# Moving the MLP's first-product weight tiles 128 bytes down in SBUF, and one slot of the other operand 384 up

## The reference, cut to what matters

```python
x = x + rms_norm(y, post_mix_norm_w[layer])
h2 = rms_norm(x, pre_mlp_norm_w[layer])
a = jax.nn.relu(jnp.einsum("bsd,df->bsf", h2, w_ff1[layer]))
m_out = jnp.einsum("bsf,fd->bsd", a * a, w_ff2[layer])
x = x + rms_norm(m_out, post_mlp_norm_w[layer])
```

## Time and profile before

| what | us |
|---|---|
| median of the runs | 2107.64 |
| the two runs | 2107.47, 2107.82 |
| span of the profiled execution | 2109.4 |
| PE busy in it | 2065.3 |
| first product, from its first matmul to the second product's first | 628.4 |
| second product, to the end of its last matmuls | 613.4 |

### The profile page before, as it was taken

One profiled execution on the slowest core, in us unless ns is written; L12 is line 12 of the kernel. 1 busy time (PEld: TensorE's weight loads), 2 busy tenths in 40 slices (PEclk: granted clock), 3 DMA queues, 4 the chain that ended last, 5 costly groups with the idle time before them and its releaser, 6 DMA issues. The chain is left out here.

```text
span 2109.4 us, 26456 instructions
## 1 busy us (share of the span) xinstructions
PE 2065.3 (98%) x9843; PEld 1719.6 (82%) x9843; DVE 1441.5 (68%) x1979; ACT 913.2 (43%) x1545; POOL 414.6 (20%) x252
## 2 busy tenths in 40 slices
PE   7999999999999999899999999999999999999998
PEld 4897878878788888688888788888788888888887
DVE  5797999989567777876667866666663536534286
ACT  5633334343445444655445644554432313313163
POOL 0000000000001322333322322332262144400012
PEclk9999999999999999999999999999999999999999
DMA  5031212113656865854455655445766455443376
GB/s 201 11 101 51 70 40 77 54 30 107 195 165 205 264 225 167 269 175 136 153 164 179 235 165 157 138 145 172 254 227 249 163 206 187 167 167 137 140 250 219
DMA packets 253118, 338.53 MB, mean 160 GB/s; under 512 B 11584, under 2 KB 193600, under 8 KB 239168
## 3 DMA queue, kind: packets, MB, share of 16 engines
q1 hardware_dynamic: 220352, 315.80, 44.9%
q10 hardware_dynamic: 32384, 20.98, 3.1%
q0 software_dynamic: 256, 0.07, 0.0%
HBM read 225.58 MB, written 111.21 MB: 160 GB/s over the span
## 5 line engine op out<-in xcount | busy, mean ns | idle before, releaser
L1861 PE MATMUL psum<-x_hi,w_hi_P 128*128 128x512 f32 x896 | 350.5, 391 | 12.3 <-DVE x_lo L1805 6.2
L2079 PE MATMUL psum<-w_hi,hid_hi 128*128 128x512 f32 x896 | 349.3, 390 | 2.0 <-DVE hid_lo L1957 2.0
L1861 PE MATMUL psum<-x_lo,w_hi_P 128*128 128x512 f32 x896 | 349.6, 390 | 0.0
L1861 PE MATMUL psum<-x_hi,w_lo_P 128*128 128x512 f32 x896 | 349.5, 390 | 0.0
L2079 PE MATMUL psum<-w_lo,hid_hi 128*128 128x512 f32 x896 | 349.3, 390 | 0.0
L2079 PE MATMUL psum<-w_hi,hid_lo 128*128 128x512 f32 x896 | 349.1, 390 | 0.0
L1957 DVE TENSOR_TENSOR hid_lo<-hid_raw,hid_hi 128x1024 fp32r<-128x1024 f32 x112 | 176.7, 1615 | 207.4 <-ACT hid_hi L1952 207.3
L1774 POOL TENSOR_TENSOR w_raw<-w_raw 128x512 f32<-128x512 f32 x128 | 181.5, 1439 | 410.7 <-DVE w_lo_P L1787 388.5
L1952 ACT ACTIVATE hid_hi<-hid_raw 128x1024 fp32r<-128x1024 f32 x112 | 113.0, 1051 | 342.6 <-DMA hid_raw<-scratch_hid 342.6
L1787 DVE TENSOR_TENSOR w_lo_P<-w_raw,w_hi_P 128x512 fp32r<-128x512 f32 x224 | 184.6, 836 | 107.2 <-ACT w_hi_P L1783 104.2
L1783 ACT ACTIVATE w_hi_P<-w_raw 128x512 fp32r<-128x512 f32 x224 | 136.8, 627 | 255.7 <-PE psum L1861 249.3
(11 more groups left out here) (280 smaller groups left out, 3762.0 us busy)
## 6 DMA issues: line engine op xcount, KB each, us to landing
scratch_hid<-stage SPq DMA_DIRECT2D x224, 256.0 KB, 3.6
hid_raw<-scratch_hid SPq DMA_DIRECT2D x56, 1024.0 KB, 4.9
w_raw<-in_w SPq DMA_DIRECT2D x52, 1024.0 KB, 5.0
w_grain<-in_w SPq DMA_DIRECT2D x48, 512.0 KB, 5.0
x_raw<-scratch_h2s SPq DMA_DIRECT2D x14, 1024.0 KB, 8.5
w_raw<-in_w_in SPq DMA_DIRECT2D x22, 512.0 KB, 3.6
scratch_h2s<-h2s SPq DMA_DIRECT2D x8, 1280.0 KB, 9.2
scratch_qk<-qout ACTq DMA_DIRECT2D x16, 512.0 KB, 3.0
```

The lines of the kernel that those rows point to most:

```text
L1861: mm = nc.tensor.matmul(psum[:, bank_1(op, g), :], l, r, start=kt == 0 and i == 0, stop=kt == 3 and i == 2)
L2079: mm = nc.tensor.matmul(psum[:, bank, :], l, r, start=f == 0 and k == 0, stop=f == NFP - 1 and k == 2)
```

## The change

Two numbers of the placement change. The 14 weight tiles of the first product move down by 1/8 KB, to remainder 0 modulo 512. Slot 7 of the tokens moves up by 3/8 KB, to remainder 0 as well; its high, low and raw tiles move together. The other seven slots and everything else stay. The tiles' order, sizes and contents are the same, and so are all instructions, waits and transfers on every engine, in number and in order.

```diff
-    x_at = [203.5, 0, 32, 16, 48, 105, 121, 167]
+    x_at = [203.5, 0, 32, 16, 48, 105, 121, 167 + 3 / 8]
     x_hi = [at(f"x_hi{i}", kb, (4, TB), F32R) for i, kb in enumerate(x_at)]
     x_lo = [at(f"x_lo{i}", kb + 8, (4, TB), F32R) for i, kb in enumerate(x_at)]
     x_raw = [at(f"x_raw{i}", kb + 8, (4, TB)) for i, kb in enumerate(x_at)]
-    w1_hi = {op: at(f"w1_hi_{op}", 69 + 2 * i, (4, P), F32R) for i, op in enumerate(OPS)}
-    w1_lo = {op: at(f"w1_lo_{op}", 83 + 2 * i, (4, P), F32R) for i, op in enumerate(OPS)}
+    w1_hi = {op: at(f"w1_hi_{op}", 68.875 + 2 * i, (4, P), F32R) for i, op in enumerate(OPS)}
+    w1_lo = {op: at(f"w1_lo_{op}", 82.875 + 2 * i, (4, P), F32R) for i, op in enumerate(OPS)}
```

## The result

| | before | changed |
|---|---|---|
| median of the runs, us | 2107.64 (2107.47, 2107.82) | 2121.36 (2119.62, 2123.10) |
| span of the profiled execution, us | 2109.4 | 2121.3 |
| first product, first matmul to L2079's first, us | 628.5 | 641.4 |
| second product, us | 613.3 | 611.8 |

The changed kernel is slower: the record's ratio to before is 1.0057, with a 95% interval of 1.0041 to 1.0073 (two runs of each; the quotient of the two medians is 1.0065). The profiled execution of the changed kernel is the one timed at 2123.10. The interval is clear of no change, and the whole of it is under 2%. The forecast was 2100.9 us, so its sign is wrong; 2121.36 lies just above the range, at the time that rival B gave (2120.6).

What follows compares the result with a forecast made beforehand. The prediction took PE's matmuls as the bound. It summed -6.7 us for unequal remainders, 0 for slot 7 and 0 for the writers, taking the median of 2107.64 to 2100.9 us, with a range of 2096 to 2106.

Steps and rivals of the forecast that it cites:

- rival B: First product: matmuls of seven slots with unequal remainders stay at 232 ns, 13.0 us more, 2120.6 us; chance 0.20.
- The bound: Whole kernel: PE, busy 2065.3 of 2109.4 us, so time can only come from its matmuls or waits on PE.
- The 13.5 ns a matmul "there are": First product: the most a matmul could gain; being faster by 2% would need 15.7 ns, so chance 0.01.
- part (1): First product: 14 weight tiles to remainder 0 make 2496 matmuls unequal, each 2.7 ns cheaper, 6.7 us off.
- Rival A: First product: addresses at this granularity don't matter, steps stay at 226.8 ns, total 2107.6 us; chance 0.28.
- Rival C: First product: steps of 216 ns, stage 600.2 us, total 2078 us; chance 0.12.
- Part (2): First product, P1 in block 1: slot 7 moves with its weights, distance stays 0, 192 matmuls at 0 change.
- Part (3): Writers of weights and slot 7: other addresses, effects hidden behind PE; slot 7's load priced at 0, at most 1 us.
- Part (4): What is late next: the weights' chain can follow a faster PE and the seam moves along; nothing subtracted.

Runs made afterwards that it cites:

- padw32: Kernel before with half of phase A's pad behind the low weights, which lie 128 bytes lower; median 2114.21 us, ratio 1.0031.
- w64: Kernel before with all 14 weight tiles of the first product at remainder 64, slots at 128; median 2116.98 us, ratio 1.0031.
- hi0_lo128: Kernel before with the high weight tiles at remainder 0, the low ones and all slots left at 128; median 2124.40 us, ratio 1.0070.
- w0_x128: Kernel before with only the weights' half of the change: weight tiles at remainder 0, slot 7 at 128; median 2122.45 us, ratio 1.0063.
- w96: Kernel before with all 14 weight tiles of the first product at remainder 96, slots at 128; median 2124.99 us, ratio 1.0068.
- w128_x0: Kernel before with only the slot's half of the change: slot 7 at remainder 0, weights at 128; median 2110.61 us, ratio 1.0005.
- padw0: Kernel before with phase A's whole pad behind the low weights, which lie 256 bytes lower; median 2109.88 us, ratio 1.0002.
- hid256: Kernel before with one of three stationary slots of the second product, high and low, moved up 256 bytes; median 2110.86 us, ratio 1.0007.
- hid128: Kernel before with one of three stationary slots of the second product, high and low, moved up 128 bytes; median 2113.17 us, ratio 1.0021.
- x384: Kernel before with slot 7 at remainder 384, weights at 128; a single run, 2109.63 us.

## Why the prediction was wrong, point by point

- **The bound** was read rightly. The time went where PE's steps are, in L1861, and L2079's step and the writers hold what they held. The waits stayed small.
- **What an address can give or take.** The 13.5 ns a matmul "there are" for a gain are shown by no run. An estimate of mine from steps comes near them: half of the 426 ns of a step at half clock is 213, which is 13.8 under 226.8; and 18 steps of L413's 256 columns take 361.95 - 359.79 = 2.16 us, 120.0 ns each, so that 256 columns more take 106.8 ns and, if all columns cost alike, 226.8 - 2 x 106.8 = 13.2 ns do not grow with the width. What the runs showed is that no address tried gave 512 columns a regular step under 226.7. Unequal remainders took it to 232.5 here, left it at 426 ns at half clock, and changed it by 2.1 to 6.6 ns in L1861, L2079, L423, L404 and L413 when a tile moved by 128 bytes.
- **The step that failed** is in part (1): "I take -2.7, since those rows are the only ones in which the remainders differ." No run shows the 2.7 ns. L396 streams 264 columns, and no row has that width at equal remainders throughout, so its 120.8 ns (2.90 us for 24 steps) have nothing of their own width to be compared with. From the other widths a step of 264 columns at equal remainders can be estimated, at 106.8 / 256 = 0.417 ns a column: 120.0 + 8 x 0.417 = 123.3 ns, 2.5 above the 120.8. Nor do its steps follow the distance: in L396's repeating pattern of 24 steps, where the remainders agree modulo 256 (the first kt) three steps take 357 ns, and 128 bytes apart (the fifth) 358. And width decides the sign: padw32 shows 256 columns getting cheaper by 2.1 ns from a distance of 128 and 512 columns dearer by 4.3 to 6.6, in one execution. So the sum of some 13 ns that the two widths seem to have in common at equal remainders need not be the same for both at unequal ones. Measured in place of the -2.7 ns: +5.8 (232.5 against 226.7), 14.5 us more where 6.7 less were summed; it is above rival B's 5.2 too.
- **Rival B** had the condition (unequal remainders), the place, the sign and nearly the price. Its picture is only partly borne out: the stage does not stay in the irregular steps that follow a disturbance (232 in the earlier trace rows) but runs in dear patterns that repeat as exactly as the cheap one. That these cost 232.5 to 233.3, so near to 232, was in part luck: block 1 of w64 settles at 229.0. What I held against B was L396 once more.
- **Rival A** falls for moves of 32 to 128 bytes (229.0 to 233.3 ns) and holds for 256 and 512 (226.7). **Rival C** falls: no run shows a step of 216 ns or the gain behind its 2078 and 600.2 us. With the weights at 0 a step takes 232.5 ns, and 226.7 in P1 of block 1, where the tokens are at 0 as well.
- **Part (2)**, slot 7, was right in kind: with distance 0 it keeps 226.7. Settling after the unequal product before it costs 0.3 us over all 16 groups.
- **Part (3)** was right: nothing of the writers shows (VectorE is busy 1442.6 us and was 1441.5, ScalarE 911.9 and 913.2; PE waits 0.9 us for L1783 and did 1.3). **Part (4)** left out what the seam itself can vary by: a wait of 1.55 us in place of 1.98, without the half-clock steps, took 1.5 us off the second product.

In all runs it is the place of the one operand against the other that counts: moving only stationary tiles costs (hi0_lo128, w0_x128 in block 1 and w96: 233.3 ns at a granted clock of 1.00), moving only a stream's slot costs (w128_x0: 233.3 in P1), and moving both together does not (226.7 in P1 of block 1 of the changed kernel). Why the place counts no run shows; nor was it tried why the steps settle at 226.7 ns in the one case and at one of several dearer values in the other.

## What to carry to other kernels

Put both operands of every float32r matmul of 512 columns at the same remainder modulo 256 bytes, down to the low parts that serve one load in three (4.3 ns a matmul in L423). In this kernel 32 bytes off cost as much as 128, 5.8 to 6.6 ns on 226.7, 2.6 to 2.9%. When reading a trace, take the distance of starts over a few dozen matmuls: a step of 231 to 233 ns where 226.7 can be had is the sign (229 in one block of w64), and busy shares (98% in both kernels) hide it. Do not carry a price from a narrow stream to a wide one: 128 bytes off took 2.1 ns from 256 columns and put 4.3 to 6.6 on 512.

## What the runs showed that was not expected

- The settled step is the same to the digit wherever remainders agree modulo 256 (10.88 us for 48 in padw0, in hid256 and in hid128's unmoved slots), and the dear ones too come to few values: 11.20 us for 48 in hi0_lo128, w96, w32 and in block 0 of w64, 11.16 in the changed kernel and hid128.
- The period is 256 bytes, not 512: at a distance of 256 the step is 226.7 ns (x384, padw0, hid256), at 128 it is not.
- At a distance of 64 bytes two blocks of one execution run at 233.3 and 229.0 ns.
- With 256 columns a distance is a gain (117.9 against 120.0 ns). It is not put to use here, since L423 and L404 read the same tiles and lose more (6.6 and 1.2 us against 1.4). With L396's 264 columns it is no gain: its 24 steps take 2.91 us in padw32, 2.90 before.
